# Feed-forward stages on input not yet divided by its root mean square, in a hybrid SSD and HGRN2 encoder layer

## What is computed

```python
def rmsnorm(x, w):
    xf = x.astype(jnp.float32)
    y = xf * lax.rsqrt(jnp.mean(xf * xf, axis=-1, keepdims=True) + EPS)
    return (y * w.astype(jnp.float32)).astype(x.dtype)

def swiglu(h, w_gate_up, w_down):
    g, u = jnp.split(h @ w_gate_up, 2, axis=-1)
    return (jax.nn.silu(g) * u) @ w_down
...
        h = h + 0.5 * swiglu(rmsnorm(h, ffn1_norm[l]), ffn1_w_gate_up[l], ffn1_w_down[l])
        h = h + hybrid_mixer(rmsnorm(h, mix_norm[l]), w_in[l], ssd_conv_w[l], ...)
        h = h + 0.5 * swiglu(rmsnorm(h, ffn2_norm[l]), ffn2_w_gate_up[l], ffn2_w_down[l])
    return rmsnorm(h, final_norm)[:, N_META:]
```

## Time and profile before

| | |
|---|---|
| median of 3 runs | 2535.94 us (2533.18 to 2542.76) |
| profiled execution | 2537.11 us, its span 2535.6 us |
| mean granted TensorE clock | 0.977 |
| TensorE busy | 2378.0 us, 94% |
| DVE, ACT, POOL busy | 897.4, 831.0, 787.2 us |
| DMA | 144.22 MB, mean 57 GB/s |

### The profile page before, as it was taken

How to read it: one execution, slowest core, us unless ns; L and a number is a source line. 1 busy time by engine, 2 the same in 40 slices (tenths; PEclk the granted TensorE clock), 3 DMA queues, 4 the chain that set the end, 5 groups by cost and what they waited for, 6 DMA issues and landing times.

```text
span 2535.6 us, 35934 instructions
## 1 busy us (share of the span) xinstructions
PE 2378.0 (94%) x13672; PEld 2042.9 (81%) x13672; DVE 897.4 (35%) x1300; ACT 831.0 (33%) x972; POOL 787.2 (31%) x434
## 2 busy tenths in 40 slices
PE   4999999998879889999999999998998999999996
PEld 3888888887767767788888888877886888888885
DVE  5101101013867878642555555543223111011113
ACT  3331111122224324241555555543213331121222
POOL 2232223223334323333433333322333222233221
PEclk9999999999889999999999999999998999999999
DMA  2222122213101101113211111112231222212121
GB/s 77 66 64 60 58 63 62 63 57 104 42 26 34 33 25 41 33 51 108 67 42 42 38 38 41 42 34 59 78 120 47 61 58 66 64 56 70 58 60 64
DMA packets 251286, 144.22 MB, mean 57 GB/s; under 512 B 4752, under 2 KB 247616, under 8 KB 251216
## 3 DMA queue, kind: packets, MB, share of 16 engines
q1 hardware_dynamic: 248880, 130.73, 18.3%
q0 software_dynamic: 2336, 12.58, 1.4%
HBM read 133.86 MB, written 9.44 MB: 57 GB/s over the span
## 4 chain that ended last, share of the span: by engine, by line
PE 71%; issue 12%; DVE 10%; POOL 3%; ACT 2%; DMA 1%; SPq 0%; DVEq 0%; POOLq 0%; ACTq 0%
PE slot L406 62%; DVE ca L1218 2%; POOL wlo L1544 2%; PE aux L542 1%; PE aux L651 1%; PE aux L528 1%; POOL q L1664 1%; PE aux L512 1%; PE aux L538 1%; DVE e L1300 1%; DVE sq L1074 1%; PE aux L619 1%; PE aux L644 1%; PE aux L632 1%; PE aux L480 0%
## 5 line engine op out<-in xcount | busy, mean ns | idle before, releaser
L1544 POOL TENSOR_TENSOR wlo<-raw,whi 128x1024 fp32r<-128x1024 f32 x218 | 539.8, 2476 | 1337.9 <-ACT whi L725 1337.9
L406 PE MATMUL slot<-xh,whi 128*128 128x512 f32 (+2 forms) x2704 | 720.3, 348 | 50.4 <-ACT xh L742 29.5
L406 PE MATMUL slot<-xh,wlo 128*128 128x512 f32 (+2 forms) x2704 | 706.1, 343 | 0.0
L406 PE MATMUL slot<-xl,whi 128*128 128x512 f32 (+2 forms) x2704 | 698.6, 341 | 0.0
L406 PEld LDWEIGHTS slot<-xh,whi 128*128 128x128 f32 x2704 | 510.0, 191 | 128.6 <-issue 35.8
L406 PEld LDWEIGHTS slot<-xh,wlo 128*128 128x128 f32 x2704 | 515.2, 191 | 60.8
L406 PEld LDWEIGHTS slot<-xl,whi 128*128 128x128 f32 x2704 | 511.9, 190 | 59.4
L725 ACT ACTIVATE whi<-raw 128x1024 fp32r<-128x1024 f32 x241 | 253.6, 1052 | 301.6 <-PE slot L406 289.3
L1097 DVE TENSOR_TENSOR prod<-gate,slot 128x784 f32<-128x784 f32 (+1 forms) x44 | 42.4, 963 | 617.5 <-PE slot L406 617.5
L406 PE MATMUL slot<-ah,whi 128*128 128x272 f32 (+1 forms) x704 | 181.7, 340 | 0.0
L406 PE MATMUL slot<-ah,wlo 128*128 128x272 f32 (+1 forms) x704 | 181.7, 340 | 0.0
(11 more groups left out here) (252 smaller groups left out, 2492.4 us busy)
## 6 DMA issues: line engine op xcount, KB each, us to landing
raw<-in_ffn_w_gate_up SPq DMA_DIRECT2D x88, 512.0 KB, 3.8
raw<-in_w_in SPq DMA_DIRECT2D x81, 512.0 KB, 3.9
raw<-in_ffn_w_down SPq DMA_DIRECT2D x32, 448.0 KB, 3.6
raw<-in_ffn_w_down SPq DMA_DIRECT2D x16, 512.0 KB, 3.8
raw<-in_ssd_w_proj SPq DMA_DIRECT2D x8, 512.0 KB, 3.8
raw<-in_hg_w_proj SPq DMA_DIRECT2D x8, 512.0 KB, 3.7
raw<-in_w_out SPq DMA_DIRECT2D x8, 512.0 KB, 3.9
h_spill<-h POOLq DMA_DIRECT2D x1, 3072.0 KB, 9.8
```

The lines of the kernel that those rows point to most:

```text
L406: mm = pe.matmul(slot[b][:, PC + u:PC + v], w[b][:, t, :], x[:, t, u + off:v + off], start=(t == 0 and p == 0 and q == 0), stop=(t == k - ...
L1544: pool.tensor_tensor(wlo[s % 2][:, :, :], raw[s % 2][:, :, :], whi[s % 2][:, :, :].bitcast(F32), ALU.subtract).then_inc(w_lo, 1)
```

## The change

The feed-forward stages no longer normalise their input in full. xh and xl are made from h times the norm weight, without rs. Since rs is one number for each row, and rows are columns here, the gate and up results are each multiplied by it instead: DVE writes t = gate * rs out of PSUM, ACT takes SiLU of t in place, DVE multiplies t by rs again (that is the up result's factor), and the product with the up result follows as before.

In the first stage the scaled copies are made in two halves of the columns (0 to 272 and 272 to 784), and the first two jobs run as half jobs in turn (`opening`): both on the first half, then the sum of squares, then both on the second half. The squares of x are taken over the rows as they were loaded, with ACT's row sum; a diagonal matrix of these sums, multiplied by ones, spreads them over the partitions. All seven row tiles have buffers and semaphores of their own and are loaded at once, ahead of and between the first two weight tiles; the 16 vector loads are issued from ACT's queue instead of SP's. In the second stage xh and xl are made tile by tile behind each output projection job, the norm_sum stands between the first and the second job of the stage, and rms after it. The mixer's normalisation stays. Semaphore counts that follow from this are left out below.

```diff
             for n, (src, r, k, _) in enumerate(X_TILES):
-                if n >= 2:
-                    sp.wait_ge(x_mm, n - 1)
-                sp.dma_start(f1["io"][n % 2][0:k, :], src[r:r + k, :]).then_inc(x_in[n % 2], 16)
-                if n < 2:
-                    load(FFNS[0][3][:, D_FF * n:D_FF * n + P], KT, n)
+                sp.dma_start(f0["x"][n][0:k, :], src[r:r + k, :]).then_inc(x_in[n], 16)
+                if n in (2, 4):
+                    load(FFNS[0][3][:, D_FF * (n // 2 - 1):D_FF * (n // 2 - 1) + P], KT, n // 2 - 1)
...
+                    if n == 0 and j0:
+                        job(KT, xh, xl, c0, 0, jg, ready=(fx_hi, fx_lo, 2 * KT + 1), late=True)
+                        norm_sum(3, c0)
+                        job(KT, xh, xl, c0, 0, jg + 1)
...
+            def turned(n):
+
+                k = X_TILES[n][2]
+                pe.wait_ge(x_in[n], 16)
                 if n >= 2:
                     pe.wait_ge(x_ok, n - 1)
                 for t in range(KT):
-                    mm = pe.transpose(slot[n % 2][:, P * t:P * t + k], f1["io"][n % 2][0:k, P * t:P * (t + 1)], ident[0:k, 0:k])
+                    mm = pe.transpose(slot[n % 2][:, P * t:P * t + k], f0["x"][n][0:k, P * t:P * (t + 1)], ident[0:k, 0:k])
                 mm.then_inc(x_mm, 1)
-            pe.wait_ge(vec_ok, 1)
-            norm_sum(0, 0)
+
+            for n in range(3):
+                turned(n)
+            pe.wait_ge(vec_in, 16 * 16)
+            pe.transpose(aux[3][:, 0:P], f0["va"][:, :], ident[:, :])
+            pe.transpose(aux[3][:, P:P + 6 * KT], f0["vb"][:, :], ident[0:6 * KT, 0:6 * KT]).then_inc(vec_mm, 1)
+            for n in range(3, len(X_TILES)):
+                turned(n)
             pe.wait_ge(x_ok, len(X_TILES))
-            ffn(0, f1, 0, 0, 0)
+
+            def opening(b, u, v, base):
+
+                low_ready(pe, b)
+                for w, x, ready in ((whi, xh, fx_hi), (wlo, xh, fx_hi), (whi, xl, fx_lo)):
+                    for t in range(KT):
+                        pe.wait_ge(ready, base + t + 1)
+                        mm = pe.matmul(slot[b][:, PC + u:PC + v], w[b][:, t, :], x[:, t, u:v],
+                                       start=(w is whi and x is xh and t == 0), stop=(x is xl and t == KT - 1))
+                return mm
+
+            for b in range(2):
+                opening(b, 0, SPLIT, 0)
+            for n, (_, _, k, t) in enumerate(X_TILES):
+                pe.wait_ge(dg_ok, n + 1)
+                mm = pe.matmul(aux2[0][:, PC + t:PC + t + k], ones[0:k, :], f0["dg"][0:k, n, 0:k], start=True, stop=True)
+            mm.then_inc(norm_mm, 1)
+            for b in range(2):
+                opening(b, SPLIT, NT, KT).then_inc(dense_done, 1)
+            ffn(0, f1, 0, 0)
...
+            def scaled(h, w, t, u, v):
+
+                act.activation(xh[:, t, u:v], h[:, t, u:v], ACT.Copy, scale=norm_w[w][:, t:t + 1]).then_inc(fx_hi, 1)
+
+            def ffn(j0, m, c0, r, nf):
                 for n, f, k, jg, jd in ffn_groups(j0):
-                    with act.Fori(0, k) as i:
-                        split(jg + 1, 2, i)
-                        act.wait_ge(slot_free[(jg + 1) % 2], lin((jg + 1) // 2, 1, i))
-                        read_out(jg, 2, i, m["t"][:, c0:], ACT.Silu, c0)
+                    def pair(i):
+                        if i is not None or n:
+                            split(jg + 1, 2, i)
+                        act.wait_ge(slot_free[jg % 2], lin(jg // 2 + 1, 1, i))
+                        act.activation(m["t"][:, c0:], m["t"][:, c0:], ACT.Silu).then_inc(gs_ok, 1)
                         split(jg + 2, 2, i)
                         act.wait_ge(slot_free[(jg + 1) % 2], lin((jg + 1) // 2 + 1, 1, i))
-                        act.activation(m["ah"][:, bass.ds(i, 1), c0:], m["p"][:, c0:], ACT.Copy).then_inc(a_hi_ok, 1)
+                        act.activation(m["ah"][:, slice(0, 1) if i is None else bass.ds(i, 1), c0:], m["p"][:, c0:], ACT.Copy).then_inc(a_hi_ok, 1)
+
+                    if n == 0:
+                        if j0:
+                            split(jg + 1)
+                            rms(r - 1, c0)
+                        pair(None)
+                    with act.Fori(0 if n else 1, k) as i:
+                        pair(i)
...
+            def squared(n):
+                k = X_TILES[n][2]
+                act.wait_ge(x_in[n], 16)
+                if n:
+                    act.wait_ge(ss_ok, n)
+                act.activation(f0["xs"][0:k, :], f0["x"][n][0:k, :], ACT.Square, accum_out=f0["ss"][0:k, n:n + 1]).then_inc(ss_ok, 1)
+
+            for n in range(3):
+                squared(n)
+            split(0)
+            act.wait_ge(x_ok, 3)
+            act.wait_ge(vecs_ok, 1)
+            for t in range(KT):
+                scaled(f1["h"], "ffn1", t, 0, SPLIT)
+            for n in range(3, 5):
+                squared(n)
+            split(1)
+            for n in range(5, 7):
+                squared(n)
+            act.wait_ge(x_ok, len(X_TILES))
+            for t in range(KT):
+                scaled(f1["h"], "ffn1", t, SPLIT, NT)
+            rms(0, 0)
             act.wait_ge(lb_sub, 1)
             act.activation(lbs[:, 1:3, :, :], lbs[:, 1:3, :, :], ACT.Exp).then_inc(lb_exp, 1)
             act.activation(aneg[:, :], alog[:, :], ACT.Exp).then_inc(lb_exp, 1)
-            for n, (_, _, k, t) in enumerate(X_TILES):
-                if n == 0:
-                    split(0)
-                act.wait_ge(x_ok, n + 1)
-                if n >= 2:
-                    act.wait_ge(acc_ok, n)
-
-                act.activation(x_sq[:, n % 2, :, 0:k], f1["h"][:, :, t:t + k],
-                               ACT.Square).then_inc(sq_ok, 1 + (n == len(X_TILES) - 1))
-            rms(0, 0)
+            ffn(0, f1, 0, 1, 0)
...
-            down(f2, N_META, J_WO, 3, True)
-            rms(3, N_META)
-            normed(2, N_META)
-            ffn(J_FF2, f2, N_META, 4)
+            for t in range(KT):
+                split(J_WO + t + 1)
+                act.wait_ge(slot_free[(J_WO + t) % 2], (J_WO + t) // 2 + 1)
+                scaled(f2["h"], "ffn2", t, N_META, NT)
+                square(f2["h"][:, t, N_META:], t % 2, 3, N_META, t)
+            ffn(J_FF2, f2, N_META, 4, D_FF // P)
...
+            def low_scaled(h, w, t, u, v, n):
+
+                dve.wait_ge(fx_hi, n)
+                dve.scalar_tensor_tensor(xl[:, t, u:v], h[:, t, u:v], norm_w[w][:, t:t + 1], xh[:, t, u:v].bitcast(F32),
+                                         ALU.mult, ALU.subtract).then_inc(fx_lo, 1)
+
             def ffn(j0, m, c0, r, nf):
+                dve.wait_ge(rs_ok, r)
                 for n, f, k, jg, jd in ffn_groups(j0):
                     with dve.Fori(0, k) as i:
                         b = (jg + 1) % 2
-                        dve.wait_ge(slot_free[jg % 2], lin(jg // 2 + 1, 1, i))
+                        dve.wait_ge(dense_done, lin(jg + 1, 2, i))
+                        dve.tensor_tensor(m["t"][:, c0:], slot[jg % 2][:, PC + c0:], rs[:, c0:], ALU.mult).then_inc(slot_free[jg % 2], 1)
+                        dve.wait_ge(gs_ok, lin(nf + f + 1, 1, i))
+                        dve.tensor_tensor(m["t"][:, c0:], m["t"][:, c0:], rs[:, c0:], ALU.mult).then_inc(gr_ok, 1)
+                        dve.wait_ge(gr_ok, lin(nf + f + 1, 1, i))
                         dve.wait_ge(dense_done, lin(jg + 2, 2, i))
                         dve.wait_ge(a_ok, lin(nf + f, 1, i))
                         dve.tensor_tensor(m["p"][:, c0:], m["t"][:, c0:], slot[b][:, PC + c0:], ALU.mult).then_inc(slot_free[b], 1)
...
+            for n in range(3):
+                copied(n)
+            dve.wait_ge(const_ok, 1)
             dve.wait_ge(vec_mm, 1)
-            own.add(dve.tensor_copy(vec_a[:, :], aux[0][:, 0:P]))
-            one(dve.tensor_copy(vec_b[:, :], aux[0][:, P:P + 6 * KT]))
+            own.add(dve.tensor_copy(vec_a[:, :], aux[3][:, 0:P]))
+            dve.tensor_copy(vec_b[:, :], aux[3][:, P:P + 6 * KT]).then_inc(vecs_ok, 1)
+            own.wait()
+            dve.wait_ge(vecs_ok, 1)
+            for n in range(3):
+                diagonal(n)
+            for n in range(3, len(X_TILES)):
+                copied(n)
+                for t in range(2 * n - 6, 2 * n - 4):
+                    low_scaled(f1["h"], "ffn1", t, 0, SPLIT, t + 1)
+            for n in range(3, len(X_TILES)):
+                diagonal(n)
+            for t in range(KT):
+                low_scaled(f1["h"], "ffn1", t, SPLIT, NT, KT + t + 1)
...
-            down(f2, N_META, J_WO, 3, True, 1.0)
-            normed(f2["h"], "ffn2", 3, 2, N_META)
+            for t in range(KT):
+                j = J_WO + t
+                hm = f2["h"][:, t, N_META:]
+                dve.wait_ge(dense_done, j + 1)
+                dve.scalar_tensor_tensor(hm, slot[j % 2][:, PC + N_META:], 1.0, hm, ALU.mult, ALU.add).then_inc(slot_free[j % 2], 1)
+                dve.wait_ge(slot_free[j % 2], j // 2 + 1)
```

(24 more changed lines are left out.)

87 lines of the change are left out of this document (33 added, 54 removed).

## The result

| | before | after |
|---|---|---|
| median of four runs, taken side by side (us) | 2534.56 (2531.20 to 2542.76) | 2490.51 (2489.86 to 2492.29) |
| profiled execution (us), its span | 2537.11, 2535.6 | 2490.41, 2488.6 |
| ratio after to before, 95% interval | | 0.9819 (0.9806 to 0.9832) |

A forecast was written before the change was run, and what follows sets the result against it. TensorE was taken as the bound, so only stretches where it waits could gain: opening 25.3 plus passage 19.9 make 45.2 us, from 2537.1 to 2491.9, or 2490.7 against the median. Forecast 2491, range 2483 to 2501.

The forecast's parts named there:

- the likeliest case: Whole kernel: opening and passage into the second stage both gain as costed, 2491 us, own range 2486 to 2496; chance 0.68.
- The loops cost nothing: Gate and up loops: 88 new VectorE instructions cost 0; chain after a gate job 5.4 us, slack 3.0.
- Rival 4: Loops: slack is not there, each excess us costs 43; about 2526 at half price, 2560 at full; chance 0.03.
- The passage: Last output-projection job to second job of stage two: 18.9 us against 38.82, 19.9 us gained.
- The gap of 0.5: Behind job J_FF2 + 1: TensorE waits once for the next weights' low part; chain 8.9 us, job hides 8.4.
- The stated reason: Passage: its time came from TensorE's stop and the half clock after it; norm_sum 2.93 us against 1.56 later.
- The opening: Start to first-stage up product: 24.2 + 17.1 + 1.7 + 3.0 = 46.0, plus 0.3 wait; 25.3 us gained from 71.6.
- Small loads: Opening: the last of the 16 loads on the scalar queue lands at 12 us, bounds 9.8 to 16.
- The collision with GpSimd: Opening: two VectorE low halves wait out GpSimd's weight subtraction, moving the last row copy from 22.4 to 24.5; 24.2 taken.
- The clock's term: Opening: after about 4 us stopped, TensorE begins half jobs at 1.2 GHz; 0 to 6.0 us added, 3.0 taken.
- The second rival: Opening: scalar queue bounds it, through issues at twice SP's cost or small loads at 16; 2495 to 2502; chance 0.17.
- The third rival: Opening: cheap issues, no GpSimd collision, no half clock; half jobs end at 39 to 41; 2484 to 2486; chance 0.09.

The follow-up runs named there:

- the control: The changed kernel itself, unchanged, measured again on the chip of the later runs beside it: 2491.50 us, ratio to before 0.9815.
- the five copies: Changed kernel with five extra scalar-engine copies ahead of each gate's SiLU in both feed-forward stages: 2576.14 us.
- two-copy run: Changed kernel with two extra scalar-engine copies ahead of each gate's SiLU: 2497.34 us; a first run of it took 4978.79 us.
- a: Changed kernel with only the six norm-vector loads on the scalar queue, the other ten small loads behind the rows on SP: 2489.22 us.
- b: Changed kernel with eleven identity transposes filling TensorE's stop ahead of the first half jobs: 2491.31 us.
- a and c: Changed kernel with only six norm-vector loads on the scalar queue and row tiles 3 to 6 transposed into other PSUM banks: 2484.05 us, ratio to before 0.9787.

## Why the prediction was right, step by step

The time came out 0.5 us from the forecast, the likeliest case was the one that happened, and each of its two sums was within 1 us of its mark. Part of that is luck: terms that cancelled, told below, and marks that move from one execution to the next (the up product stood at 46.45 in this trace and at 45.11 in the control's). By the medians the gain is 44.05 us where 45.2 was forecast.

**The loops cost nothing.** Right, with its size: chain 5.4 forecast, 5.3 measured, slack 3.0 forecast, 2.9 to 3.2 by the five copies. A pair of jobs takes 17.15 us against 17.14. Rival 4 would have needed 1.05 us a round; none showed, and the two-copy run shows that even 1.8 us more in the chain costs the rounds nothing. It also shows that the first round of each stage has less slack than the rest. The forecast had counted both, with 0.3 and 0.5; what came was 0 and 0.39.

**The passage.** 18.9 forecast, 18.18 measured: job, norm_sum 1.45 at full clock (1.56 taken), job. The gap of 0.5 was 0.39 us, but it stands behind the up product that I measured to, so it had no place in that sum; it shows in the next pair instead (1936.87 - 1919.34 = 17.53 us against 16.88), the 0.7 that the second stage gives back. The stated reason, that most of the gain is the stop and the clock that falls with it, holds: 12 of the 20.6 us were stops of TensorE and 8 the slower clock (the result's section), and in the run that puts the wait back 7.2 us of waits cost 11.8.

**The opening: 46.0 (46.3 with the wait) forecast, 46.45 measured**, from terms that were off in both directions:
- Issue on the scalar engine's queue, 6.6 taken as on SP, took 7.8 (1.05 to 8.84). Small.
- Small loads landed at 14.5, not 12, inside the bounds of 9.8 to 16. The last was issued at 8.37 and ended 5.7 us after that was done, where it took 2.2 with only the other small loads issued ahead of it. The Trainium skill (DMA: Bandwidth & Descriptors, Queues, rings and completion order) says that each DMA engine goes round the queue rows in turn, a packet at a time. By that they need not wait behind the rows; the trace doesn't bear that out in full. They landed when the row and weight loads, which moved 400 GB/s from 7 to 10 us and 338 from 10 to 13, were nearly over. With only the six norm vectors on that queue, issued from 1.05 to 3.4, tile 3 was turned at 9.78 instead of waiting on them at 14.5. In the same run the ten other small loads stood behind the rows on SP's own queue and took 5.0 to 6.6 us from issue to landing, so the delay isn't one of the second queue alone. Whether it is the queue's turn, the number of small packets or something else stays open: no run tells them apart.
- From there to the first copy 3.0 us, as said (2.8); then a copy each 1.96 us, not 2.14, 0.5 less in all.
- The collision with GpSimd ahead of the last copy was costed at 1.8 and didn't come in this trace: GpSimd started at 22.60, just behind VectorE's 22.54, and was itself slowed to 3.06. It came in four others: two low halves took 3.00 us (1/rms awaited in the opening), 2.78 (a), 2.99 (two copies) and 3.00 (five copies) instead of 0.89, with the last copy some 2 us later. In a GpSimd had begun first; in the other three it began 0.33 to 0.35 us behind the first of the two. Where it began 0.01 to 0.28 us behind, in six traces, VectorE lost nothing and GpSimd took 2.84 to 3.12 us. So the term is right in size, and whether it comes is a matter of a few tenths in when both start.
- 2.7 late, 0.5 and 1.8 early: last copy ended at 24.57 where 24.2 was said.
- Half jobs from 24.62 to 46.25, 21.6 us, of which the clock 2.5 (3.0 taken), the sum over the diagonals 1.68 (1.7). The clock's term was the middle of 0 and 6.0; b measures it, and in the control the same first half jobs took 7.72 us, 1.0 less. Its reason did not hold as given: a stop of about 4 us was forecast and read against the rows, but TensorE stood 2.76, less than the 3.13 after which the earlier trace rows shows full clock, and the clock fell all the same, to 0.50 from 23.5 to 30 us. Size right, partly by luck.
- 1/rms was ready at 38.4 (38), and the up product did not wait.

**The rivals.** The second rival's mechanism was there in a mild form (small loads 2.5 us late), and the missed collision covered it. Both came in the runs with two and five copies, where the first half job began at 26.39 and 26.36 instead of 24.62; so both together are worth some 1.8 us more, a time of about 2492, and not yet this rival's 2495. The third rival asked for an earlier last copy, no collision and no half clock; runs a and c are that case made on purpose, 37.93 for the 39 to 41 it gave.

**GpSimd beside VectorE.** In the opening two low halves took 2.78 to 3.00 us instead of 0.89 beside a GpSimd subtraction in four traces; in the loops nothing was lost, since the multiply ends at 75.15 and GpSimd starts at 75.16. The Trainium skill (GPSIMD Engine Reference, Key points) names contention with VectorE instructions that have two SBUF inputs; the opening agrees, and in the loops the order of the work keeps the two apart.

## What to carry to other kernels

A division by a row's norm can go behind a matmul over that row, and its worth is then the stop that TensorE no longer makes plus the time at half clock behind that stop: here 7.2 us of waits cost 11.8. New work in a loop is free up to its measured slack (a few dummy operations give it to some 0.3 us), but check the first round of each stage by itself, where the chain starts later. When an opening is rearranged, look for the bank or buffer that ties the first matmul to the last load: here that edit and another, which had the first matmuls wait for fewer small loads, were worth 7.5 us more together.

## What the runs showed that I had not expected

- The last of the small loads on a second hardware queue landed 5.7 us after its issue was done, with 338 to 400 GB/s going through the first; it took 2.2 us where only small loads had been issued ahead of it, and 4.8 behind the large loads on their own queue (run a).
- A square with a row sum is followed by an instruction that reads the accumulator, 0.19 us, at a pitch of 1.24 us for the pair (1.06 and 0.15 were taken).
- Issuing on the scalar engine's queue takes 0.28 to 0.85 us of that engine's time for each load, 7.8 us for 16.
- Of TensorE's clock: it was at half after stops of 2.76 (two traces), 3.54, 4.01 and 5.98 us, and at full after 1.56 us and after 3.13; after 2.76 us in another trace of the same program, and 2.75 in a fourth, it fell only behind the first products. The length of a stop alone does not tell it.
- How long TensorE is at half clock differs from one execution to the next (the mixer's norm_sum took 2.98 and 1.75 us in two of one program), and a stretch that no edit touched by up to 4.2 us between traces (1854.47 to 1858.71). An edit worth less than that is told by its marks, not by the time.
